# The 32 position bias loads of an encoder block: issued by ScalarE in three groups instead of by SyncE

## The reference

```
proj = x @ w_in                        # 1024 x 4608: q, k, v, u, v of the gating unit, two gates
y_na = neighbourhood_attention(q, k, v, rpb)      # 8 heads of 64, 4 rows x 64 columns of tokens
y_sg = spatial_gating(gelu(su), gelu(sv), ...)
merged = sigmoid(ga) * (y_na @ w_branch_na) + sigmoid(gb) * (y_sg @ w_branch_sg)
x = layer_norm(ALPHA * x + merged @ w_out)
x = layer_norm(ALPHA * x + peer(x))    # 8 heads x 16 of 16384 single-neuron experts
```

## Time and profile before

| | us |
|---|---|
| median of 3 runs | 1122.9 |
| lowest and highest | 1122.12, 1127.78 |
| the profiled execution | 1127.2 |
| its span in the profile | 1125.4 |
| busy: TensorE, VectorE, ScalarE, GpSimd | 1027.9, 834.7, 450.0, 424.2 |
| TensorE's mean granted clock | 0.958 of full |

### The profile page before, as it was taken

The page is one execution under the profiler, slowest core; times in us unless marked ns, Lnnn a source line. Parts: engine busy times, 40 slices in busy tenths (PEclk is TensorE's granted clock), DMA queues, the critical chain, the costliest instruction groups (busy, mean ns, idle before and its releaser), DMA issues.

```text
span 1125.4 us, 20306 instructions
## 1 busy us (share of the span) xinstructions
PE 1027.9 (91%) x6766; PEld 941.7 (84%) x6766; DVE 834.7 (74%) x1474; ACT 450.0 (40%) x645; POOL 424.2 (38%) x278
## 2 busy tenths in 40 slices
PE   7879999799999999999999999108999999999995
PEld 6758899699999999999999999107888888888884
DVE  3246647757999999888888888007888888888887
ACT  4246444334343434444444444003444444444442
POOL 0310000003888888878888888870000000000000
PEclk9889999799999999999999999658999999999998
DMA  7675579672666565978777775227777777777773
GB/s 244 180 244 191 185 262 301 226 259 42 148 131 149 132 141 139 205 168 170 168 168 171 169 169 108 0 4 254 239 243 242 237 244 241 240 242 240 243 242 129
DMA packets 154863, 211.22 MB, mean 188 GB/s; under 512 B 55888, under 2 KB 103760, under 8 KB 154832
## 3 DMA queue, kind: packets, MB, share of 16 engines
q1 hardware_dynamic: 117968, 210.68, 59.6%
q0 software_dynamic: 36864, 0.15, 8.9%
HBM read 192.81 MB, written 17.96 MB: 187 GB/s over the span
## 4 chain that ended last, share of the span: by engine, by line
PE 43%; POOL 36%; issue 8%; DVE 5%; DMA 3%; SPq 3%; ACT 1%; POOLq 0%; DVEq 0%; ACTq 0%
POOL expert_weights L441 36%; PE ps L1232 31%; PE ps L1157 10%; DMA w_raw<-in_w_in_dram 3%; SPq L291 2%; DVE w_lo L869 1%; PE ps L1055 1%; ACT w_hi L549 1%; PE ps L1033 0%; DVE xres L669 0%; DVE xres L676 0%; PE ps L1043 0%; DMA expert_weights<-gw,cell 0%; DVE small L657 0%; DVE v_lo L949 0%
## 5 line engine op out<-in xcount | busy, mean ns | idle before, releaser
L441 POOL DMA_INDIRECT expert_weights<-gw,cell x256 | 408.3, 1595 | 272.5 <-DVE gw L862 192.8
L1190 PE MATMUL ps<-act_hi,uT_hi 128*128 128x256 f32 x1024 | 295.1, 288 | 0.0
L1190 PE MATMUL ps<-act_hi,uT_lo 128*128 128x256 f32 x1024 | 289.9, 283 | 0.0
L1190 PE MATMUL ps<-act_lo,uT_hi 128*128 128x256 f32 x1024 | 289.7, 283 | 0.0
L623 ACT ACTIVATE v_hi<-v_raw 128x512 fp32r<-128x512 f32 x256 | 147.9, 626 | 257.5 <-PE ps L1232 198.8
L1232 PE MATMUL ps<-v_hi,hid_hi 128*128 128x512 f32 x512 | 158.7, 391 | 56.5 <-DVE v_lo L949 56.5
L1190 PEld LDWEIGHTS ps<-act_hi,uT_hi 128*128 128x128 f32 x1024 | 196.6, 192 | 0.0
L1190 PEld LDWEIGHTS ps<-act_lo,uT_hi 128*128 128x128 f32 x1024 | 196.6, 192 | 0.0
L1190 PEld LDWEIGHTS ps<-act_hi,uT_lo 128*128 128x128 f32 x1024 | 196.3, 192 | 0.0
L949 DVE TENSOR_TENSOR v_lo<-v_raw,v_hi 128x512 fp32r<-128x512 f32 x256 | 164.9, 686 | 0.3 <-ACT v_hi L623 0.3
L1232 PEld LDWEIGHTS ps<-v_hi,hid_hi 128*128 128x128 f32 x512 | 96.4, 189 | 77.0 <-issue 57.1
(11 more groups left out here) (146 smaller groups left out, 1378.4 us busy)
## 6 DMA issues: line engine op xcount, KB each, us to landing
v_raw<-in_peer_v_dram SPq DMA_DIRECT2D x128, 512.0 KB, 4.2
u_raw<-in_peer_u_dram SPq DMA_DIRECT2D x68, 512.0 KB
u_raw<-in_peer_u_dram SPq DMA_DIRECT2D x240, 128.0 KB
w_raw<-in_w_in_dram SPq DMA_DIRECT2D x8, 2048.0 KB, 12.2
expert_weights<-zeros SPq DMA_DIRECT2D x16, 1024.0 KB, 12.3
g_in<-expert_weights SPq DMA_DIRECT2D x128, 128.0 KB, 3.0
w_raw<-in_peer_wq_dram SPq DMA_DIRECT2D x4, 2048.0 KB, 10.8
w_raw<-in_w_out_dram SPq DMA_DIRECT2D x2, 2048.0 KB, 8.7
```

The costliest lines, as they stand in the source:

```text
L441: pool.indirect_dma_start(out=table_cells, out_offset=bass.IndirectOffsetOnAxis(ap=cell[:, t, k:k + 1], axis=0), in_=gw[:, t, k:k + 1], in ...
L1190: ins = pe.matmul(ps[:, bank, 0:T], (uT_hi, uT_hi, uT_lo)[part][:, slot, k, :], (act_hi, act_lo, act_hi)[part][:, k, :], start=(k == 0 and ...
```

## The change

The function `load_bias` moves from SyncE's program to ScalarE's, word for word but for the engine that issues. SyncE's call behind chunks 1, 2 and 3 goes; ScalarE calls it at half chunks 1, 2 and 3, behind everything else that it does there.

```diff
@@ block.sync
-        def load_bias(group):
-            for h in range(*BIAS_HEADS[group]):
-                for r in range(ROWS):
...
-                    sp.dma_start(dst, src).then_inc(s[f"rpb_in{group}"], 16)
...
-            if 1 <= c <= len(BIAS_HEADS):
-                load_bias(c - 1)
@@ block.scalar
+        def load_bias(group):
+            for h in range(*BIAS_HEADS[group]):
+                for r in range(ROWS):
+                    at = (h * RPB_H + WIN_H - ROWS + r) * RPB_W + WIN_W - GRID_W
+                    src = bass.AP(na_rpb.tensor, na_rpb.offset + at,
+                                  [[1, GRID_W], [RPB_W, ROWS], [1, GRID_W]])
+                    b, p0 = r // 2, GRID_W * (r % 2)
+                    dst = bias[p0:p0 + GRID_W, h, b, :].rearrange("p (r c) -> p r c", r=ROWS)
+                    act.dma_start(dst, src).then_inc(s[f"rpb_in{group}"], 16)
...
             if hc == 3:
                 copy_constants()
+            if hc - 1 in range(len(BIAS_HEADS)):
+                load_bias(hc - 1)
```

## The result

| | before | changed |
|---|---|---|
| median, us | 1124.27 (19 runs) | 1129.78 (19 runs) |
| lowest and highest, us | 1122.12, 1128.19 | 1127.76, 1132.79 |
| ratio | | 1.0046, 95% interval 1.0036 to 1.0056 |
| span of the profiled execution, us | 1125.4 | 1127.0 |

The change made the kernel 0.46% slower, about 5.2 us by the ratio and 5.5 by the medians. The time lies in the range that was forecast (1114 to 1138). The forecast of +2.4 us had the sign and a little under half of the size. It was added to 1122.9, the median of 3 runs; that of all 19 is 1.4 us higher, so that 1.4 of the 4.5 us between 1125.3 and 1129.78 are the base and 3.1 the change.

A forecast was written before the change was run, and what follows sets the result against it. Bound: mostly TensorE and GpSimd, with SyncE's bias issues delaying weight chunks in the first 110 us. 14.4 - 9.0 - 3.8 + 2.4 = +4.0 at half chunk 8, then -2.4 + 0.8: +2.4 on 1122.9, 1125.3 us; range 1114 to 1138.

The forecast's parts named there:

- the exchange: First 80 us: SyncE's late chunks go (9.0 us of waits), ScalarE's w_hi comes late (half chunk 4 14.4 us later).
- Group 1: ScalarE's first 8 bias loads, behind w_hi of half chunk 1: fit in 8.2 us of room, cost nothing.
- group 2: ScalarE's 12 loads behind the copy of q: 10.2 us, ending at 35.9; TensorE idles 8 us before half chunk 3.
- Price of an issue: ScalarE's time per bias load, bounds 0.66 and 1.80 us; 10.2 us taken for the second twelve, 13.2 for the third.
- the floor: Least time per issue, 0.66 us, from SyncE's shortest 616 ns plus 0.04 us between two.
- The third group: ScalarE's 12 loads behind the constants' copies, at 1.10 us each: 13.2 us, ending at 52.0; half chunk 4 at 56.3.
- rival D: Bias packets and SyncE's chunk share DMA engines, holding ScalarE 1.47 us an issue: +14.3 us, 1137.2 us; chance 0.25.
- forecast A: The main forecast, ScalarE's issues at 0.75 to 1.15 us each: 1125.3 us, spanning 1119 to 1130; chance 0.48.
- The low clock: TensorE at part speed after a wait: 2.4 us added at half chunk 4, 3.8 us saved at 4 to 6.
- one to one: Behind half chunk 9 TensorE, routing and scatter have no slack, so the +2.4 us shift reaches the end whole.
- B: ScalarE issues at 0.66 us each, its queue being its own and short: -6.2 us, 1116.7 us; chance 0.15.
- C: Issuing costs ScalarE nearly nothing, so all TensorE's early waits go: -18.5 us, 1104.4 us; chance 0.12.

The follow-up runs named there:

- the held kernel without loads: No bias loads (zeros instead), but ScalarE held at the same places by 4, 7 and 7 idle copies; 1129.86 us, ratio 1.0050 to the kernel before.
- quarter loads: Changed kernel with each of the 32 loads bringing only its first 64 of 256 elements a partition; 1112.76 us, ratio 0.9888 to the kernel before.
- strips: One contiguous 157-element strip a partition instead of four pieces of 64: on the kernel before (SyncE issues) 1104.88 us, on the changed kernel (ScalarE issues) 1114.26 us.

## Why the prediction was nearly right

**Path.** The step that forecast the exchange (SyncE's stalls go, ScalarE's w_hi of half chunks 3 and 4 comes late, three waits become two) stands in the profile, and the held kernel without loads shows that a hold of ScalarE's queue is enough to give the whole time, to within about 1 us. Group 1 cost nothing in the end, as forecast. But the 21.9 that the working allowed for w_hi of half chunk 2 was read from the execution with the slow start; in this one q ended 2 us earlier, w_hi came at 20.87, and TensorE waited 0.9 us. That wait is lost in the hold of group 2 behind it.

**Price of an issue, the step that was off.** The second group took 15.07 us, not 10.2: I had let five of its twelve go at the floor because ScalarE's queue would be empty. It was not empty. The last load of the first group had not landed before 33.28, when GpSimd could start to mask it:

```profile
33.28 4.14 POOL L411 TENSOR_SCALAR_AFFINE_SELECT bias<-bias 64x768 f32<-64x768 f32 x4 [30.53 <-DMA bias<-in_na_rpb_dram]
```

And chunk v was in flight until 34.2. The first issue took 0.60 us and the next eight 0.9 to 1.9 each. No run tells the group's own queue from the chunk there. The other seven were priced at 0.99, from nine issues that were read as nearly alone; they had the tail of chunk v beside them too, until 37.51. The third group took 16.4 us, not 13.2, beside chunk sv, and for that group the run with sv held back shows the chunk to be the reason (11.7 us without it). That is rival D's mechanism, at 1.26 and 1.37 us rather than the 1.47 that D was priced at. The mean of the two groups, 1.31 us, lies outside the 0.75 to 1.15 of the forecast A. Together this is +8.1 us.

**What came off.** ScalarE's sequencer runs ahead of its computing: the third group began at 38.91, with w_hi of half chunk 3 just started at 38.83, and not behind it and the copies. Of these 2.9 us I had allowed 1, in the lower bound. And the second group began at 23.66, 2.0 us before its time, by the better start of this execution. So w_hi of half chunk 4 was due at 52.0 and came at 55.43, 3.4 us later; the terms give 4.9 + 3.2 - 2.9 - 2.0 = 3.2.

**Behind it.** From the start of half chunk 4 to that of 8 I had 27.4 us; it took 86.0 - 59.8 = 26.2. The low clock behind the wait cost 1.0 us (72 matmuls in 18.08 us, where three times 5.70 is 17.1) and not the 2.4 that I had taken from the old half chunk 8. Half chunk 8 came 6.3 us later than before (forecast 4.0), half chunk 10 at 101.81 and not 97.24, 4.6 later. 1.7 us were given back, as forecast (1.6). From there the shift stays at 4.6 us for seventeen half chunks. It falls to the 3.4 of the first scatter in one place, where TensorE was at the lower clock for less long than before. These are 16.3 us from the start of half chunk 26, first row before, second after:

```profile
218.70:235.00 16.30, 16.30 (x114) 16.30 (x115) 0.81 0.59 193
```

```profile
223.20:239.50 16.30, 16.28 (x123) 16.30 (x123) 0.89 0.59 192
```

That is 9 matmuls more in the same time, 1.1 us. So the shift went on "one to one", as forecast, up to there. Why the clock was low for less long is open.

**Luck.** Put into the sum of the prediction, the measured price of an issue gives 2.4 + 8.1 = +10.5 us, 1133.4: still in the range, but clearly slower. That the change cost 5.5 us is due to three things that were not in the sum: the sequencer running ahead (2.9, of which 1 was in the lower bound), the shorter way from half chunk 4 to 8, mostly by less low clock (1.2), and the clock at half chunk 26 (1.1). That these took away 5 of the 8 us was luck. The measured 0.46% stands just inside the 0.5% within which I had put 0.50, next to the 0.32 for slower, and its interval (0.36 to 0.56%) lies on both sides of that line.

**Rivals.** B (issues at the floor) is true of quarter loads and strips, not of these loads. C (an issue costs nothing) is refuted by ScalarE's own rows, idle for 14.16 and 13.93 us behind its issues. The held kernel shows what such a hold is worth: take it away and the ratio falls from 1.0050 to 0.9821, some 25 us. By the Trainium skill (DMA: Bandwidth & Descriptors, "Issuing engines are not separate DMA queues") the DMAs of all engines run on the same 16 DMA engines and interleave; chunks landing after 15.1 us beside ScalarE's loads, and 8.4 without, agree with it. The same section of the Trainium skill says that the time to initiate a DMA is usually small relative to the DMA itself. One issue, 1.26 or 1.37 us, is small beside the 8.4 us that a bias load took to land (the median in the changed kernel). Twelve in a row, 15.07 and 16.42 us, are not.

## What to carry to other kernels

Before moving DMA issues from one queue to another, ask what stands behind them in each: the same 32 issues cost 25 us ahead of two roundings that TensorE waits for, and 13 us spread one head at a time. Look at the packets first. Here a load of 256 pieces of 256 bytes held its queue for 1.3 us (ScalarE) to 1.5 us (SyncE) on average, and the big transfers beside such loads landed later. The same data in 64 strips of 628 bytes cost nothing that the intervals show, from the engine that had them all along. A stall that is visible on one engine is only an upper bound of the gain, since the next engine in the chain may be held as long.

## What the runs showed of the hardware

- An issue of a load of 64 pieces takes ScalarE 0.62 us in the median (quarter loads; the shortest 0.47). The shortest of a full load's 256 pieces takes 0.60 us on ScalarE and 0.62 on SyncE.
- One queue's loads make issues on the other long. The load of a norm weight took SyncE 7.33 us to issue while ScalarE's bias loads were in flight (19.76 to 27.09), and 0.50 us in the run without bias loads. ScalarE's issues of 3.47 and 2.73 us came right behind SyncE's issue of sv at 43.09.
- ScalarE's sequencer starts to issue DMAs before the ACTIVATE ahead of them is done (11.37 against 11.79 to 13.73).
- After a wait of 12 us TensorE's mean granted clock was 0.65 in the next 8.8 us, and after one of 8 us 0.81 in the next 8.2. The run without bias loads kept 1.00 from 25.7 to 53.9.
